# One tile less of lead for VectorE's half of a weight split

## The reference

```
h = rms_norm(x);  z, xbc, dt, q, k, v, g_ssd, g_att = split(h @ w_in)      # 1024 x 7440
y_ssd = ssd(z, xbc, dt) @ w_ssd_out;  y_att = attention(q, k, v) @ w_attn_out
x = x + (sigmoid(g_ssd) * y_ssd + sigmoid(g_att) * y_att) @ w_out
x = x + moe(rms_norm(x))                 # 32 experts, weights of 96 MB in fp32
x = rms_norm(x + sigmoid(rms_norm(x) @ w_ple_gate) * (p @ w_ple))
h = rms_norm(x);  hy_in, z_hy, c_q, c_kv, k_rope, z_attn, gates = split(h @ w_in_2)
u_hy = (hyena(hy_in) * silu(z_hy)) @ w_hy_out
u_attn = (attention2(c_q @ w_uq, c_kv @ w_ukv) * silu(z_attn)) @ w_attn_out_2
out = x + (g_hy * u_hy + g_at * u_attn) @ w_out_2
```

## Time and profile before

| | before |
|---|---|
| median of three runs | 797.02 us (796.76 to 798.28) |
| the profiled execution | 796.26 us |
| its span, first to last instruction | 794.5 us |
| TensorE matmuls, busy | 738.9 us (93%) |
| TensorE weight loads, busy | 557.4 us (70%) |
| VectorE, busy | 465.0 us (59%) |
| ScalarE, busy | 321.6 us (40%) |
| mean granted clock of TensorE | 0.972 |

### The profile page before, as it was taken

How to read it: one execution, slowest core, us unless ns; L and a number is a source line. 1 busy time by engine, 2 the same in 40 slices (tenths; PEclk the granted TensorE clock), 3 DMA queues, 4 the chain that set the end, 5 groups by cost and what they waited for, 6 DMA issues and landing times.

```text
span 794.5 us, 11035 instructions
## 1 busy us (share of the span) xinstructions
PE 738.9 (93%) x4636; PEld 557.4 (70%) x4636; DVE 465.0 (59%) x825; ACT 321.6 (40%) x479; POOL 17.9 (2%) x15
## 2 busy tenths in 40 slices
PE   7999999999999999996799798779999999999998
PEld 7978886888877886563345254337999966678886
DVE  6878965455766665531333221128777698875673
ACT  6464446536437225210111110127674634255631
POOL 0000000000000000000000000001100003000000
PEclk9999999999999999998879988899999999999999
DMA  9765542333439849899999999997453654433311
GB/s 314 238 206 185 163 158 104 106 107 106 139 110 410 294 189 422 315 366 420 419 421 417 421 421 421 419 398 268 148 197 120 214 184 160 156 109 106 106 53 54
DMA packets 63153, 189.97 MB, mean 239 GB/s; under 512 B 7481, under 2 KB 11835, under 8 KB 51132
## 3 DMA queue, kind: packets, MB, share of 16 engines
q1 hardware_dynamic: 61326, 184.44, 62.7%
q10 hardware_dynamic: 1774, 4.79, 1.8%
HBM read 188.16 MB, written 1.05 MB: 238 GB/s over the span
## 4 chain that ended last, share of the span: by engine, by line
PE 64%; DVE 14%; DMA 13%; ACT 6%; issue 2%; POOL 1%; SPq 0%; DVEq 0%; POOLq 0%
PE pb L519 60%; DMA raw<-in_w_exp_up 6%; DMA WHo<-in_w_exp_up 4%; DVE rawo L1785 4%; PE pb L528 4%; ACT WH L1282 2%; DMA WHo<-in_w_exp_down 1%; DVE cv_ L1893 1%; ACT arena L1441 1%; DVE arena L2054 1%; DMA X<-in_x 1%; POOL small L2690 1%; DVE arena L2100 0%; ACT arena L1476 0%; ACT arena L1310 0%
## 5 line engine op out<-in xcount | busy, mean ns | idle before, releaser
L1785 DVE TENSOR_TENSOR rawo<-raw,WH 128x2048 fp32r<-128x2048 f32 (+5 forms) x80 | 172.7, 2175 | 64.5 <-ACT WH L1282 64.4
L519 PE MATMUL pb<-WH,HTh 128*128 128x512 f32 (+2 forms) x384 | 155.0, 404 | 3.9 <-DVE rawo L1785 1.7
L1282 ACT ACTIVATE WH<-raw 128x2048 fp32r<-128x2048 f32 (+5 forms) x80 | 144.0, 1822 | 21.1 <-PE pb L519 15.1
L519 PE MATMUL pb<-rawo,HTh 128*128 128x512 f32 (+2 forms) x384 | 147.7, 385 | 0.0
L519 PE MATMUL pb<-WH,HTl 128*128 128x512 f32 (+2 forms) x384 | 147.5, 384 | 0.0
L519 PEld LDWEIGHTS pb<-WH,HTh 128*128 128x128 f32 x384 | 72.3, 188 | 22.5 <-issue 5.1
L519 PEld LDWEIGHTS pb<-rawo,HTh 128*128 128x128 f32 x384 | 72.2, 188 | 14.3
L519 PEld LDWEIGHTS pb<-WH,HTl 128*128 128x128 f32 x384 | 72.4, 188 | 13.0 <-issue 1.0
L519 PE MATMUL pb<-WH,arenao 128*128 128x512 f32 x192 | 59.7, 392 | 1.2 <-DVE arenao L1819 1.2
L519 PE MATMUL pb<-raw,arena 128*32 128x256 f32 (+1 forms) x256 | 49.7, 491 | 10.8 <-DMA raw<-in_w_exp_up 6.3
L519 PE MATMUL pb<-arena 128*32 128x256 f32 (+6 forms) x252 | 58.1, 429 | 1.6 <-ACT arena L1698 0.7
(11 more groups left out here) (363 smaller groups left out, 1266.2 us busy)
## 6 DMA issues: line engine op xcount, KB each, us to landing
raw<-in_w_in SPq DMA_DIRECT2D x46, 1024.0 KB, 5.1
raw<-in_w_exp_up SPq DMA_DIRECT2D x18, 1024.0 KB, 21.1
arena<-in_w_exp_gate SPq DMA_DIRECT2D x13, 1024.0 KB, 22.4
arena<-in_w_exp_down SPq DMA_DIRECT2D x12, 1024.0 KB, 15.8
WHo<-in_w_exp_down SPq DMA_DIRECT2D x9, 1024.0 KB, 23.5
raw<-in_w_out SPq DMA_DIRECT2D x8, 1024.0 KB, 5.2
raw<-in_w_exp_gate SPq DMA_DIRECT2D x8, 1024.0 KB, 16.0
WHo<-in_w_exp_up SPq DMA_DIRECT2D x8, 1024.0 KB, 21.4
```

Source lines behind the costliest of these rows:

```text
L519: return e.matmul(o, l, r, start=start, stop=stop, skip_group_check=True)
L1282: e.activation(h_, r_, ACT.Copy).then_inc(hi.sem, hi.mark(k))
L1785: e.tensor_tensor(l_, r_, h_.bitcast(F32), ALU.subtract).then_inc(lo.sem, lo.mark(k))
```

## The change

The lead becomes a parameter of `Splitting`: ScalarE keeps `AHEAD` = 3, VectorE gets 2. A call `weights(consumed)` on VectorE now emits the low parts up to tile `consumed + 1`, not `consumed + 2`. ScalarE, TensorE, GpSimd and SyncE have the same instructions in the same order as before, and VectorE the same instructions in another order. 55 of the 80 low parts stand at a later place than before; the other 25 stand at the same place.

```diff
@@ -474,13 +474,13 @@
         class Splitting:
-            def __init__(self):
-                self.k, self.end = 0, dense_again
+            def __init__(self, ahead):
+                self.k, self.end, self.ahead = 0, dense_again, ahead
             def due(self, consumed):
                 while self.k < self.end:
                     first = 0 if self.k < dense_again else dense_again
-                    if self.k - AHEAD >= max(first, consumed):
+                    if self.k - self.ahead >= max(first, consumed):
                         return
@@ -1268,7 +1268,7 @@
         def scalar(e):
-            splitting = Splitting()
+            splitting = Splitting(AHEAD)
@@ -1775,7 +1775,7 @@
         def vector(e):
-            splitting = Splitting()
+            splitting = Splitting(AHEAD - 1)
```

## The result

The changed kernel takes 854.83 us (median of 4 runs, 854.67 to 855.96); the kernel before, on the same chip, 796.99 us. The ratio is 1.0727, with a 95% interval of 1.0708 to 1.0746: slower by 57.8 us. The forecast was 854.0 us. The profiled execution took 854.67 us, its span is 852.9 us and its mean granted clock 0.955 (before 0.972).

What follows compares the result with a forecast made beforehand. TensorE was taken as the bound, its matmuls busy 738.9 of 794.5 us. 796.3 plus 49.0 of stalls minus 5.5 of gain, 0.7 to the median (840.5) and 13.5 for the clock gave 854 us, range 836 to 868.

Steps and rivals of the forecast that it cites:

- The wait that goes: VectorE's 64.4 us idle ahead of line 1785 goes; only 5.5 us of TensorE waits behind it count as gain.
- Low part end against first load: Per tile, end of VectorE's row ahead plus about 2.2 us, minus TensorE's first weight load, gives the stall; together 49.0 us.
- the ten large places: Stalls at tiles 3, 34, 36, 39, 45, 59, 64, 67, 68 and 77, from 2.1 to 7.0 us, together 38.0 us.
- the nine small ones: Stalls at tiles 9, 11, 13, 32, 47, 48, 52, 55 and 56, 0.2 to 2.7 us, together 10.9 us.
- The signs asked for: Some 45 us of TensorE waits for line 1785, at least 15, longest at tile 67; gap moves from tile 7 to 3.
- They add up: Stalls add rather than overlap, since each row ahead itself waits for TensorE: 49.0 us before gains.
- The experts pass it on: The expert stage does not swallow the third of the 43.5 us lost ahead of it; its stream starts later by the same.
- The rival with an absorbed start: The experts' stream hides some 15 us and two low-clock stretches lost before it: 834 us, chance 0.08.
- TensorE has no slack: In dense products loads start 0.22 us apart and last 0.19 us, so a stall moves all that follows.
- The rival that reads TensorE's headroom from the busy share of its weight loads: Weight loads busy only 70%, so TensorE's slack takes the stalls: no change, 797 us, chance 0.02.
- The clock: Half-clock stretches of 6.7 us behind five of six dense-product stalls of 3.4 to 7.0 us, 2.7 us each: 13.5 us.
- The row at 509.60: Profile stretch among the experts, 509.60 to 516.30 us, at granted clock 0.50 after a 4.28 us standstill; basis for 2.7 us.

Runs made afterwards that it cites:

- The gain alone: Kernel before with VectorE's lead of two only at chosen tiles; fastest set, all below tile 67 but twenty tiles kept at their old place: 790.98 us, ratio 0.9921.
- One place alone: Kernel before with only tile 34's low part moved, behind the two drains of line 2125: 802.44 us, ratio 1.0068.
- taking one back: Changed kernel with tile 67 alone kept at its old place in VectorE's queue: 847.76 us, ratio 1.0647.
- The two halves: Kernel before with the lead of two for tiles 0 to 41 only, 816.69 us, or for tiles 42 to 79 only, 833.59 us.
- the first half alone: Kernel before with the lead of two for tiles 0 to 41 only, those ahead of the experts: 816.69 us, ratio 1.0252.
- with 28 matmuls: Kernel before with tile 34's low part moved and 28 small TensorE matmuls ahead of the wait for it: 807.23 us, ratio 1.0125.
- 17 at tile 34: Kernel before with tile 34's low part moved and 17 matmuls by zeros ahead of the wait for it: 801.02 us, ratio 1.0044.
- ten places: Changed kernel with 8 to 30 matmuls by zeros ahead of the low-part waits of ten tiles: 841.77 us, ratio 1.0543.
- the fourth such kernel: Changed kernel with small matmuls ahead of the low-part waits of tiles 34, 36, 56, 59, 64 and 68: 856.04 us, ratio 1.0737.

## Why the prediction was right

- **The wait that goes is VectorE's and worth little.** 64.4 us fell to 1.2 us and the gain in it was about 7 us, where 5.5 were counted. I had counted by the gaps of the matmuls, and the first loads gained more than these gaps: 2.1 us for 1.67 us ahead of tile 7, 1.5 us for 1.33 us ahead of tile 20, 1.0 us for 0.67 us ahead of tile 60. The gain alone was run, and is real: 6.5 us of the median.
- **Low part end against first load.** This step carried the forecast. For the ten large places it said 38.0 us and they measured 38.9; for the nine small ones 10.9 and 11.5. Each of the ten was hit to within 0.25 us. The signs asked for came: 45 us of waits at 15 places or more (45.7 at 18), the longest at tile 67, next tile 36, the gap ahead of tile 7 gone and one ahead of tile 3. One place alone costs what it costs among the nineteen (4.1 us), and taking one back takes back its wait and no more.
- **They add up.** The two halves sum to the whole within 1 us.
- **The experts pass it on.** 20.9 us ahead of them and 20.6 us behind; 20.0 and 19.6 with the first half alone. The rival with an absorbed start is out.
- **TensorE has no slack.** A single stall in one dense product is still there 500 us later. The rival that reads TensorE's headroom from the busy share of its weight loads is out too.
- **The clock.** Right in its cause and its sum, wrong in its make-up. The term was five stretches of 6.7 us at 2.7 us each, 13.5 us. There were ten, eight of them of half that length. Eight of the ten steps were 1.3 to 1.6 us, one 0.8 us and one, behind a stretch of 6.83 us (tile 64), the 2.7 us that I had taken: 15 us. The row at 509.60, of the experts, was taken as the form of all of them; in the dense stages most were 3.41 us. I also counted stalls of 3.4 us and more alone, and in the changed kernel it fell behind those of 2.7 to 2.9 us too (tiles 3, 39, 56, 77). More stretches and cheaper ones happened to cancel, and the stalls, 1.4 us above their term, were balanced by the gain, 1.5 us above its own; so the hit of the total to 1 us is partly luck; stretches of 6.7 us behind all ten would have given 840.5 + 27 = 868 us, the edge of the range.

The Trainium skill ("TensorE: Matmul & The Clock Gate", Terms) prices throttled time at that time x (1 - K/N). Here it would be (8 x 3.41 + 2 x 6.83) x 0.5 = 20.5 us, as an estimate, against 15 us by the steps of the first loads. The trace shows a part of why at 739.05: of 6.82 us at half clock TensorE is busy for 3.62, since the stretch began inside the stall. At tiles 36, 64, 67 and 77 together 5.0 us of the stretches lie ahead of the first load, by the same formula 2.5 of the 5.5 us; the rest isn't split up.

## What to carry to other kernels

When an engine waits for its input in order to work ahead, look at who needs what it works on before taking the wait away: with in-order queues a shorter lead puts the early work behind a row that waits for the very engine it feeds, and the two then wait in turns. For each moved piece compare the end of the row that it will stand behind, plus its own duration, with the time at which it is needed; do the same for what it now stands in front of. Where the consumer is a dense TensorE chain, count a half-clock stretch behind each longer stall (here each of the 21 stalls of 3.5 to 7.1 us had one, and 11 of the 16 of 2.7 to 2.9 us), and take its price from one in such a dense chain, not from another stage; and choose the lead tile by tile: here a lead of two at the right tiles gained 0.8%, at all of them it lost 7.3%.

## What the runs showed of the hardware

The granted clock doesn't fall alike behind like stalls. Behind tile 3's stall of 2.9 us it fell in the changed kernel for 3.4 us (+1.5 us on tile 4), and in the kernel with the first half alone, which has the same instructions up to there, it did not. Over all kernels, stalls of 2.7 to 2.9 us at tiles 3, 39, 56 and 77 without small matmuls had such a stretch 11 times of 16. Behind tile 36's stall it was 3.4 us in the one and 6.8 us in the other. In the two kernels with tile 34 alone, bare and with 28 matmuls, there was a stretch of 3.4 us at 228 us, far from any edit, which cost 1.5 us, and no such stretch in the kernel before. And the experts, in which all kernels are alike, had between 34 and 48 us at half clock in the profiled runs and took from 0.3 us less to 3.1 us more than in the kernel before. The three profiles in which they took 0.9 us more or longer are all of kernels with small matmuls (17 at tile 34: 0.9, ten places: 1.3, 28 at tile 34: 3.1); in the fourth such kernel and in all the others it was 0.04 us at most. With the 3.1 us the time at half clock was the same as in the kernel before (44.4 us), so the granted clock doesn't explain it. What decides between these cases was not found out. A difference of one or two microseconds in a single profile can be this; the step at its own tile tells it from an effect of the edit.
